# The order in which a mixture-of-experts loop visits its 32 experts: by number, or experts of more than 64 tokens in turn with the others

## What is computed

```python
N_EXPERTS = 32; TOP_K = 4; D_MODEL = D_EXPERT = 1024; SEQ = 512
logits = (t @ w_router + b_router).astype(F32)
top_val, top_idx = lax.top_k(logits, TOP_K)
gate = jax.nn.softmax(top_val, axis=-1)
...
def expert_block(args):
    xb, e = args
    h = xb @ w_mlp1[e] + b_mlp1[e]          # 1024 x 2048
    glu, lin = jnp.split(h, 2, axis=-1)
    ...
    return a @ w_mlp2[e] + b_mlp2[e]        # 1024 x 1024
...
out = jnp.zeros((T, D), u.dtype).at[row_tok].add(ys * row_gate[:, None].astype(ys.dtype))
```

## Time and profile before

| | us |
|---|---|
| median of three runs | 1618.17 |
| the profiled execution | 1621.13 |
| its span, first to last instruction | 1619.3 |
| start of turn 0 of the experts' loop (line 1167) | 548.00 |
| start of turn 1, of turn 2 | 587.66, 614.02 |
| start of turn 31 | 1556.27 |
| end of the last `down` of turn 31 | 1585.30 |

### The profile page before, as it was taken

How to read it: one execution, slowest core, us unless ns; L and a number is a source line. 1 busy time by engine, 2 the same in 40 slices (tenths; PEclk the granted TensorE clock), 3 DMA queues, 4 the chain that set the end, 5 groups by cost and what they waited for, 6 DMA issues and landing times. The chain is left out here.

```text
span 1619.3 us, 35352 instructions
## 1 busy us (share of the span) xinstructions
PE 1445.9 (89%) x13337; PEld 775.2 (48%) x13338; DVE 743.4 (46%) x1772; ACT 568.4 (35%) x1078; POOL 345.5 (21%) x228
## 2 busy tenths in 40 slices
PE   5999999899996688899999899999899898999981
PEld 2788776566775234333444344334333333344430
DVE  6699977898206424223332332233223322323236
ACT  3444435754323123322233333323332333224323
POOL 4678787411650000000000000000000000000000
PEclk9999999899998899999999999999899999999996
DMA  4232221111348389999999999999999999999995
GB/s 155 79 101 94 79 91 65 53 40 40 123 142 352 120 340 412 414 397 376 366 389 415 402 416 403 413 406 414 413 405 388 412 394 404 398 393 395 415 399 226
DMA packets 50465, 475.17 MB, mean 293 GB/s; under 512 B 7936, under 2 KB 8192, under 8 KB 25856
## 3 DMA queue, kind: packets, MB, share of 16 engines
q1 hardware_dynamic: 42000, 455.71, 70.5%
q0 software_dynamic: 7280, 16.79, 2.9%
q10 hardware_dynamic: 1152, 2.24, 0.4%
HBM read 466.71 MB, written 16.78 MB: 299 GB/s over the span
## 5 line engine op out<-in xcount | busy, mean ns | idle before, releaser
L1078 PE MATMUL bank<-big,ring 128*32 128x512 f32 x4992 | 563.4, 603 | 21.3 <-issue 18.6
L1078 PEld LDWEIGHTS bank<-big,ring 128*32 128x32 f32 x4992 | 156.2, 111 | 379.8 <-issue 372.8
L1104 PE MATMUL bank<-big,mix 128*32 128x256 f32 x4992 | 298.1, 391 | 12.6 <-DMA big<-in_d_w 12.4
L1104 PEld LDWEIGHTS bank<-big,mix 128*32 128x32 f32 x4992 | 168.2, 112 | 113.3 <-DMA big<-in_d_w 15.3
L1001 POOL DMA_INDIRECT y_rows<-mix,sidx x32 | 30.4, 950 | 889.3 <-ACT mix L1037 889.3
L1037 ACT ACTIVATE mix<-bank,sgate 32x256 f32<-32x256 f32 x384 | 178.7, 465 | 69.4 <-PE bank L1104 43.4
L1025 ACT ACTIVATE ring<-ring 128x256 f32<-128x256 f32 x96 | 40.0, 417 | 463.3 <-DVE ring L1227 463.3
L472 PE MATMUL bank<-mix_r,sm_r 128*128 128x512 f32 x328 | 134.6, 410 | 17.1 <-POOL uT_r L245 10.5
L472 PE MATMUL bank<-mix_r,ring_r 128*128 128x512 f32 x344 | 136.3, 396 | 0.0
L472 PE MATMUL bank<-uT_r,sm_r 128*128 128x512 f32 x328 | 129.7, 395 | 0.0
L717 DVE SCALAR_TENSOR_TENSOR bank<-big,chan,bank 128x512 f32<-128x512 f32 x176 | 116.6, 750 | 0.0
(11 more groups left out here) (271 smaller groups left out, 1764.1 us busy)
## 6 DMA issues: line engine op xcount, KB each, us to landing
big<-in_d_w SPq DMA_DIRECT2D x192, 2048.0 KB, 19.4
ring<-in_d_dense SPq DMA_DIRECT2D x67, 512.0 KB, 3.3
big<-y_rows SPq DMA_DIRECT2D x2, 2048.0 KB, 19.8
xT<-in_d_xT SPq DMA_DIRECT2D x4, 512.0 KB, 9.3
uT<-in_d_x SPq DMA_DIRECT2D x1, 2048.0 KB, 9.5
u_rows<-xT SPq DMA_DIRECT2D x4, 512.0 KB, 16.9
xT<-y_rows SPq DMA_DIRECT2D x1, 2048.0 KB, 13.0
xT<-y_rows SPq DMA_DIRECT2D x4, 512.0 KB, 5.4
```

The costliest lines, as they stand in the source:

```text
L1078: mm = pe.matmul(halves(bank[g][c * G:(c + 1) * G, :], FC), t.xe[:, k, g * G:(g + 1) * G], cols, start=(k == 0), stop=(k == KB - 1), tile_ ...
L1104: mm = pe.matmul(bank[PY[g % 2]][c * G:(c + 1) * G, 0:FC], t.aT[:, g, x, b * G:(b + 1) * G], t.w2[:, b, x, c * FC:(c + 1) * FC], start=(b ...
```

## The change

From the counts, VectorE marks the experts 1 to 30 that have more than 64 tokens (`wide`), counts them and the others along the row (`nwide`, `nthin`), and works out for each expert its entry in the list (`turnof`): wide and thin experts in turn, a wide one first, each kind in the order of their numbers, and what is left of the more numerous kind behind. Experts 0 and 31 stay first and last. From `turnof` each partition finds which expert stands in its entry (`whose`), and this takes the place of `pnum` in columns 0 and 2. Nothing else is changed; further pieces are formed as before.

```diff
@@ -892,6 +892,22 @@
             extra, own, before, isx = (t.tmp[:, c:c + 1] for c in range(4))
             pnum = t.kf[:, K_P:K_P + 1]
+            mid = slice(1, E - 1)
+            numbers, whose, room = t.kf[:, K_E:K_E + E], t.whose[:, 0:1], t.whose[:, 1:2]
+            wide, nwide, nthin, turnof = t.wide[:, mid], t.nwide[:, mid], t.nthin[:, mid], t.turnof[:, mid]
+            total = t.nwide[:, E - 2:E - 1]
+            step.add(dve.tensor_copy(t.turnof[:, :], numbers))
+            step.link(dve.tensor_scalar(wide, t.cnt[:, mid], float((NG - 1) * G), None, ALU.is_gt))
+            step.link(dve.tensor_tensor_scan(nwide, t.kf[:, K_ONE:K_ONE + E - 2], wide, 0.0, ALU.mult, ALU.add))
+            step.add(dve.tensor_tensor(nthin, numbers[:, mid], nwide, ALU.subtract))
+            step.link(dve.tensor_scalar(room, total, -1.0, float(E - 1), ALU.mult, ALU.add))
+            step.link(dve.scalar_tensor_tensor(turnof, nthin, total, nthin, ALU.min, ALU.add))
+            step.link(dve.scalar_tensor_tensor(nwide, nwide, room, nwide, ALU.min, ALU.add))
+            step.link(dve.scalar_tensor_tensor(nwide, nwide, 1.0, turnof, ALU.subtract, ALU.subtract))
+            step.link(dve.tensor_tensor(nwide, nwide, wide, ALU.mult))
+            step.link(dve.tensor_tensor(turnof, turnof, nwide, ALU.add))
+            step.link(dve.scalar_tensor_tensor(t.turnof[:, :], t.turnof[:, :], pnum, numbers, ALU.is_equal, ALU.mult))
+            step.link(dve.tensor_reduce(whose, t.turnof[:, :], AX.X, ALU.add))
...
-            step.link(dve.tensor_scalar(own, own, float(E - 1), pnum, ALU.min, ALU.subtract))
+            step.link(dve.tensor_scalar(own, own, float(E - 1), whose, ALU.min, ALU.subtract))
...
-            step.add(dve.tensor_scalar(t.listcol[:, 0:1], own, pnum, None, ALU.add))
+            step.add(dve.tensor_scalar(t.listcol[:, 0:1], own, whose, None, ALU.add))
...
-            step.link(dve.tensor_scalar(own, own, pnum, None, ALU.add))
+            step.link(dve.tensor_scalar(own, own, whose, None, ALU.add))
```

More of the change, by code:

```diff
@@ L1431, in build @@
         t.cnt, t.more, t.run, t.below = (sb(x, [P, E]) for x in ("cnt", "more", "run", "below"))
+        t.wide, t.nwide, t.nthin, t.turnof = (sb(x, [P, E]) for x in ("wide", "nwide", "nthin", "turnof"))
+        t.whose = sb("whose", [P, 2])
         t.tmp, t.listcol, t.lists = sb("tmp", [P, 4]), sb("listcol", [P, LIST]), sb("lists", [1, LIST * P], I32)
```

## The result

| | before | changed |
|---|---|---|
| median of 20 runs each, us | 1616.5 | 1622.7 |
| the profiled execution, us | 1621.1 | 1621.4 |
| its span | 1619.3 | 1619.6 |

A forecast was written before the change was run, and what follows sets the result against it. The prediction took the loop to be bound by its loads except in the run of four wide turns. Its terms, -8.0 + 6.5 + 2.5 + 0.7 = +1.7 us, added to 1618.2 gave 1619.9 us, range 1613 to 1627.

The forecast's parts named there:

- no change to be told: Whole kernel: a time between 1613.3 and 1623.0 us, within about 0.3% (4.9 us) of before; chance 0.68.
- The loads set the pace, 32.5 us per expert: Loop: first loads of turns land 32.5 us apart whatever the mix of wide and thin turns, from a never-empty queue.
- The four wide turns had lost 8.0 us, to be won back: Turns 6 to 9 before: landings took 105.5 us for three, 8.0 us lost; the change wins up to that back.
- The second wide turn at the front, 6.5 us lost: Turn 1, now wide: landings of turns 2 to 3 take 39.0 us, 6.5 us lost, ends 2.7 and 7.7.
- the end given: Turn 1: 7.7 us, the upper end for the loss from a second wide turn at the front.
- chain of marks: Turn 1: issues and landings of pieces followed one by one, giving 38.6 us between first landings of turns 2 and 3.
- Twelve instructions, 2.5 us: VectorE before the loop: twelve instructions at 0.21 us add 2.5 us, fully exposed; ends 2.3 and 3.0.
- The store of the tokens: Block before the loop: only rival for its end, but its last issue is over 28 us earlier, so it hides nothing.
- The tail, 0.7 us: Turn 31, behind five thin turns with the queue at its fullest: 0.7 us added, ends 0 and 2.
- TensorE is the bound: Loop, rival: turns cost what TensorE takes, giving 1589 us; decides from a pace under 31.2 us; chance 6%.
- The thin turns grow: Alternating thin turns, rival: they lengthen toward 31.3 us and TensorE sets the pace, 1638 us, or 1624 at half; chance 11%.
- The bound of 29.1: Thin turns behind wide ones: the length in us from which the rival of growing thin turns would decide.

The follow-up runs named there:

- e3: The changed kernel with the comparison turned round, so a thin expert comes behind expert 0 as turn 1: 1615.6 us, 0.9994 of before.
- e9: e3 with the chain woven into the instructions for the pieces and five copies moved ahead: 1610.7 us, 0.9964 of before.
- e11: e9 with the list made from `pnum`, so by number, and the woven chain's result thrown away: 1616.9 us, 0.9994 of before.
- e2: The kernel before with the changed kernel's list taken from a constant column, without the twelve instructions: 1618.0 us, 1.0009 of before.
- e5: The kernel before with a constant-column list (two thin, 14 wide-thin pairs, two thin) and thin expert 1 loaded ahead: 1607.3 us, 0.9955.

## Why the prediction was right or wrong

The forecast was 1619.9 us, +1.7 against before; it is 1622.7, and the difference is +5.7 (4.4 to 7.0). The range of 1613 to 1627 holds it; the likeliest of the outcomes, no change to be told (0.68), is not what came, by 0.8 us; slower had 0.23.

- *The loads set the pace, 32.5 us per expert.* Right: 32.45 from turn 3 to 31 in the changed kernel, and the kernel is 3.4% faster when they are made lighter. (The share of the DMA engines falls a little at wide turns outside the run of four too, to 0.97 in the one at 1195.84 of the earlier trace rows.)
- *The four wide turns had lost 8.0 us, to be won back.* Right: with a thin turn 1 the landings from 2 to 31 take 942.1 and 943.5 us (e3, e9), about 8 less than the 949.4 to 952.1 by number. In the runs e9 is 6 us faster (3.6 to 8.2), and e11 shows that nothing but its order is.
- *The second wide turn at the front, 6.5 us lost.* The mechanism was right, the size low: 40.3 us from landing 2 to 3, 7.8 over the pace, just past the end given. The chain of marks had 38.6. Counted from the landing of turn 2's first load, the third piece landed after 14.8 us (15.5 in the chain of marks), the first `w2` piece after 27.2 (27.8) and the second after 32.8 (33.2). The last step was mis-sized: turn 3's first load came 7.5 us behind that piece, where the chain had 5.4 for every step of a full queue. Turn 1 has also a low stretch of the clock in its opening. It shifted the issues from 6.5, 22.4 and 34.7 us after the start of the turn to 8.0, 23.9 and 36.3, so the landing of turn 2's first load came as much later as the others: it doesn't show in the 40.3, but it is a loss ahead of it, for which the forecast had nothing.
- *Twelve instructions, 2.5 us.* This term was mis-sized most. The instructions take 2.60 us, but from the copy of the counts to the end of the block, and to turn 0, it is 3.2 us more in the trace: behind them TensorE turns the columns at half clock (0.6 us more). (By the clock of the trace the block's last instruction does not come later, 533.09 against 533.85, since this execution had reached the counts 4.0 us earlier.) In the runs the chain costs 4.7 and 6.0 us by its two measurements. The prediction costed TensorE's part by the length of what it waits for and did not ask at what clock the six matmuls behind it would run, though half clock was near in the trace of before (0.61 on average from 530.5 to 548.0). Why the runs give 1.5 to 2.8 us more than the trace is open; the low stretch of turn 0 is a candidate that the traces don't confirm. The store of the tokens was no rival: its last part landed at 522.4, 11 us ahead of the block's last instruction (the 28 count from its issue).
- *The tail, 0.7 us.* Nothing to speak of: from the landing at 1553.9 to the end of the last `down` at 1585.63, 31.7 us, against 31.6.
- *The rival "TensorE is the bound"* (1589) fell with the first trace. *"The thin turns grow"*: most did, to 28.4 to 29.1 us in the middle, at the 29.1 from which it would have decided, and the pace stayed at 32.45. The bound of 29.1 was not a good sign: in e2 one such turn took 29.5 and the pace stayed at 32.5, for where the loads are the bound, waits fill a thin turn up to their time.

The sum, stage by stage in the two traces, changed against before: from the copy of the counts to the start of turn 0 27.4 us against 24.2, +3.2 (forecast +2.5); from there to the landing of turn 2's first load 57.8 against 54.8, +3.0 (nothing was forecast; turn 0 and the opening of turn 1, each with its low stretch, have 1.5 each); from there to the landing of turn 31's first load 949.0 against 951.0, -2.0 (forecast -8.0 + 6.5 = -1.5); behind it +0.1 (forecast +0.7). Together +4.3, against 5.7 (4.4 to 7.0) in the runs. From the landing of turn 2's first load on, the forecast of the order was right within half a microsecond. That the whole fell into the range, with 3.0 us ahead of it unforeseen, is owed to the width of the range.

## What to carry to other kernels

Before balancing work between turns, take the landing times of one load per turn: if their pace does not change with the kind of turn, no order of turns can beat it, and only the places where the pace is broken (a queue run dry) can be won. Put the turns that free their buffers early at the places where the queue is empty, here at the front. And price a few small instructions ahead of a stage on which every engine waits by a run, not by their length alone: 2.6 us of them cost 3.2 in the traces and 4.7 to 6.0 in the runs. Woven into work that stood there anyway, they cost nothing that could be measured.

## What the runs showed of the hardware

- Small VectorE instructions on 128x30 that each wait for the one before start 0.21 to 0.23 us apart (0.26 behind one that sums along the row, 0.28 to 0.29 behind one that reads a scalar from memory, in the changed kernel); two independent rows of them in turn, each waiting for all but the last issued, start 0.09 to 0.17 us apart (e9).
- At one place of the program TensorE was granted 1.2 GHz in nine traces and more in four, after waits of 3.4 to 8.7 us and of 3.6 to 4.4 us: the length of the wait just ahead did not decide it. The same six matmuls took 1.44 us and 0.82 us. A low stretch inside a wide turn lengthened that turn by 1.4 to 1.6 us.
- A 2.1 MB load issued when the one before had just landed took 7.5 us (issued 612.2, landed 619.7) and 7.6 (624.6, 632.2) in turn 1 of the changed kernel, while the load issued right behind the first of these landed 4.9 us after it (624.6). So loads issued one at a time would be slower than the pace found, 32.45/6 = 5.4 us per load.
- In twelve of thirteen traces the first matmul of turn 1 came after 4.0 to 4.6 us of idle time on TensorE that no wait explains; in e5 it stood ahead of turns 0 (5.3) and 3 (5.8). Packets of the queue "q8 instruction" moved beside these stretches.
